# Delta rule's squared query and key lengths: two fp32r products of a rounded square and its remainder in place of one fp32 product

## What is computed

```python
def l2_norm(x):
    xf = x.astype(jnp.float32)
    return xf * lax.rsqrt(jnp.sum(xf * xf, axis=-1, keepdims=True) + EPS)
...
    qkv = jax.nn.silu(causal_depthwise_conv(jnp.concatenate([q_dn, k_dn, v_dn], axis=-1), w_conv))
    q_b, k_b, v_b = jnp.split(qkv, [DN_QK_W, 2 * DN_QK_W], axis=-1)
    q_b = l2_norm(q_b.reshape(bsz, seq, DN_HEADS, DN_KEY_DIM))
    k_b = l2_norm(k_b.reshape(bsz, seq, DN_HEADS, DN_KEY_DIM))
```

## Time and profile before

| what | value |
|---|---|
| median of 3 runs | 1245.12 us (1244.88 to 1246.83) |
| profiled execution, time | 1245.51 us |
| profiled execution, span of its instructions | 1243.8 us |
| PE busy | 1228.5 us (99%) |
| DVE busy | 688.9 us (55%) |
| ACT busy | 625.8 us (50%) |
| DMA, mean over the span | 123 GB/s |
| length loop: first sum to first key transpose | 599.10 to 630.68 us |

### The profile page before, as it was taken

How to read it: one execution, slowest core, us unless ns; L and a number is a source line. 1 busy time by engine, 2 the same in 40 slices (tenths; PEclk the granted TensorE clock), 3 DMA queues, 4 the chain that set the end, 5 groups by cost and what they waited for, 6 DMA issues and landing times.

```text
span 1243.8 us, 18228 instructions
## 1 busy us (share of the span) xinstructions
PE 1228.5 (99%) x6631; PEld 998.3 (80%) x6631; DVE 688.9 (55%) x997; ACT 625.8 (50%) x1144; POOL 65.5 (5%) x96
## 2 busy tenths in 40 slices
PE   7999999999999999999999999999999999999998
PEld 5788888888888787777788888877788888888887
DVE  4566666675665884887584565566733333332221
ACT  4577676775554766665864344453532233231221
POOL 0000000001110000000321210003000000000000
PEclk9999999999999999999999999999999999999999
DMA  9666665675553333212231223643233333343320
GB/s 351 193 204 184 202 197 174 181 222 161 161 154 103 84 90 81 68 51 69 61 93 49 56 69 102 191 148 96 72 104 101 92 93 101 101 117 105 110 84 26
DMA packets 278040, 152.41 MB, mean 123 GB/s; under 512 B 8006, under 2 KB 273375, under 8 KB 277983
## 3 DMA queue, kind: packets, MB, share of 16 engines
q1 hardware_dynamic: 273626, 149.49, 41.0%
q10 hardware_dynamic: 4356, 2.15, 0.6%
HBM read 145.31 MB, written 6.29 MB: 122 GB/s over the span
## 4 chain that ended last, share of the span: by engine, by line
PE 89%; ACT 3%; DVE 3%; DMA 3%; issue 1%; SPq 0%; DVEq 0%; ACTq 0%
PE region L1691 12%; PE region L1693 12%; PE region L1696 12%; PE tail L1691 8%; PE tail L1693 8%; PE tail L1696 8%; PE tail L1681 5%; PE tail L1683 5%; PE tail L1682 5%; DMA gates<-kept_gates 2%; PE region L1983 1%; DVE w_lo L1089 1%; PE region L2150 1%; PE region L2142 1%; DMA ada_early<-in_w_ada 1%
## 5 line engine op out<-in xcount | busy, mean ns | idle before, releaser
L601 ACT ACTIVATE w_hi<-raw 128x1024 fp32r<-128x1024 f32 (+1 forms) x177 | 197.3, 1115 | 409.2 <-PE region L1696 205.4
L1089 DVE TENSOR_TENSOR w_lo<-raw,w_hi 128x1024 fp32r<-128x1024 f32 (+1 forms) x176 | 229.2, 1302 | 202.7 <-ACT w_hi L601 201.9
L1691 PE MATMUL region<-u_hi,w_hi 128*128 128x512 f32 x640 | 158.8, 390 | 0.7 <-ACT w_hi L601 0.5
L1693 PE MATMUL region<-u_lo,w_hi 128*128 128x512 f32 x640 | 158.1, 389 | 0.0
L1696 PE MATMUL region<-u_hi,w_lo 128*128 128x512 f32 x640 | 158.1, 389 | 0.0
L1691 PEld LDWEIGHTS region<-u_hi,w_hi 128*128 128x128 f32 x640 | 119.9, 188 | 26.9 <-ACT w_hi L601 1.0
L1693 PEld LDWEIGHTS region<-u_lo,w_hi 128*128 128x128 f32 x640 | 120.2, 188 | 25.0
L1696 PEld LDWEIGHTS region<-u_hi,w_lo 128*128 128x128 f32 x640 | 120.1, 188 | 24.9
L621 ACT ACTIVATE ada_raw<-ada_raw,cond 128x128 f32<-128x128 f32 x448 | 134.1, 388 | 0.8 <-DMA ada_raw<-in_w_ada 0.8
L1681 PE MATMUL tail<-u_hi,w_hi 128*128 128x512 f32 x272 | 111.3, 409 | 2.2 <-DVE w_lo L1089 2.2
L1683 PE MATMUL tail<-u_hi,w_lo 128*128 128x512 f32 x272 | 106.3, 391 | 0.0
(11 more groups left out here) (371 smaller groups left out, 1639.2 us busy)
## 6 DMA issues: line engine op xcount, KB each, us to landing
raw<-in_w_ffn_in SPq DMA_DIRECT2D x168, 256.0 KB, 3.4
ada_raw<-in_w_ada SPq DMA_DIRECT2D x56, 512.0 KB, 4.6
raw<-in_w_in SPq DMA_DIRECT2D x90, 256.0 KB, 3.3
raw<-in_w_ffn_out SPq DMA_DIRECT2D x32, 384.0 KB, 4.5
raw<-in_w_ffn_out SPq DMA_DIRECT2D x32, 320.0 KB, 3.7
ada_early<-in_w_ada SPq DMA_DIRECT2D x8, 1024.0 KB, 9.7
gates<-kept_gates SPq DMA_DIRECT2D x16, 256.0 KB, 4.1
raw<-in_w_out SPq DMA_DIRECT2D x16, 256.0 KB, 3.3
```

The costliest lines, as they stand in the source:

```text
L601: act.activation(w_hi[:, slot % 2, 0:k, :], raw[:, slot, 0:k, :], ACT.Copy).then_inc(hi_ready, 1)
L1089: dve.tensor_tensor(w_lo[:, slot % 2, 0:k, :], raw[:, slot, 0:k, :], w_hi[:, slot % 2, 0:k, :].bitcast(f32), ALU.subtract).then_inc(lo_rea ...
L1691: pe.matmul(bank(b), w_hi[:, slot, n, :], x_hi[:, x0 + n, :], start=start and n == 0, stop=False)
L1693: pe.matmul(bank(b), w_hi[:, slot, n, :], x_lo[:, x0 + n, :], start=False, stop=False)
```

## The change

ACT rounds each square into an fp32r tile (`l2_hi`: `acc_hi` for even r, one half of a new tile `sq_pair` for odd r). DVE subtracts to get the remainder (`l2_lo`: `acc_lo`, or the other half of `sq_pair`). PE multiplies both by the fp32r ones and adds them up in the same bank. `acc_hi` and `acc_lo` served the modulation vector, whose last round is over by then.

```diff
--- before.py
+++ after.py
@@ -170,6 +170,7 @@
         gate_col = sb("gate_col", [P, 3, KD])
         ada_acc = sb("ada_acc", [P, 4, P])
         acc_hi, acc_lo = sb("acc_hi", [P, 4 * P], f32r), sb("acc_lo", [P, 4 * P], f32r)
+        sq_pair = sb("sq_pair", [P, 2, S], f32r)
         eps = sb("eps", [P, 1])
         share = sb("share", [P, 1])
         tok = sb("tok", [P, 4, NB])
@@ -259,6 +260,14 @@
         def sq_low(n):
 
             return att_hi.rearrange("p e n -> p (e n)")[:, (2 + n % 2) * S:(2 + n % 2) * S + S]
+
+        def l2_hi(r):
+
+            return sq_pair[:, 0, :] if r % 2 else acc_hi[:, :]
+
+        def l2_lo(r):
+
+            return sq_pair[:, 1, :] if r % 2 else acc_lo[:, :]
 
         def parts_of(s):
 
@@ -917,6 +926,8 @@
                     if r >= 2:
                         act.wait_ge(l2_stat, r - 1)
                     act.activation(work[:, r % 2, :], conv[:, L2[r], :], ACT.Square).then_inc(l2_sq, 1)
+                    act.wait_ge(l2_sq, r + 1)
+                    act.activation(l2_hi(r), work[:, r % 2, :], ACT.Copy).then_inc(half_hi, 1)
 
             for m in range(DNH):
                 both = (2 * m, 2 * m + 1)
@@ -1488,6 +1499,10 @@
             fill = filler(mixed)
             tmp = prod[:, 0].rearrange("p h e -> p (h e)")
             for m in range(DNH):
+                for r in (2 * m, 2 * m + 1):
+                    dve.wait_ge(half_hi, 2 * SBH + r + 1)
+                    dve.tensor_tensor(l2_lo(r), work[:, r % 2, :], l2_hi(r).bitcast(f32), ALU.subtract)\
+                        .then_inc(half_lo, 1)
                 fill("l2" if m else "silu")
                 for r in (2 * m, 2 * m + 1):
                     rs, cc = flat(link, r % 2), L2[r]
@@ -2050,10 +2065,12 @@
             for m in range(DNH):
                 fill("l2" if m else "silu")
                 for r in (2 * m, 2 * m + 1):
-                    pe.wait_ge(l2_sq, r + 1)
+                    pe.wait_ge(half_hi, 2 * SBH + r + 1)
                     if r >= 4:
                         pe.wait_ge(l2_rs, 3 * (r - 4) + 1)
-                    pe.matmul(bank(r % 4), ones[:, :], work[:, r % 2, :], start=True, stop=True).then_inc(l2_stat, 1)
+                    pe.matmul(bank(r % 4), ones_r[:, :], l2_hi(r), start=True, stop=False)
+                    pe.wait_ge(half_lo, 2 * SBH + r + 1)
+                    pe.matmul(bank(r % 4), ones_r[:, :], l2_lo(r), start=False, stop=True).then_inc(l2_stat, 1)
                 if m in (1, 2):
                     v_transposes(range(2 * m - 2, 2 * m))
             fill("start")
```

## The result

The changed kernel takes 1254.58 us (median of 6 runs, 1252.44 to 1255.74), the kernel before in the same session 1245.59 us (6 runs, 1244.70 to 1246.96). The ratio is 1.0066, 95% interval 1.0055 to 1.0076: 0.55 to 0.76% slower. The forecast was 1251.3 us with a range up to 1253.8; the measured median lies 0.8 us above the range. The profiled execution of the changed kernel, 1252.44 us with a span of 1250.7, was the quickest of the six, so its trace may show less of the loss than the median holds.

What follows compares the result with a forecast made beforehand. PE, busy 99%, was taken as the bound. Less PE work (-3.1 us), two old gaps gone (-1.0) and new standing (+10.2) made +6.1, so 1251.3 us, range 1248.5 to 1253.8.

Steps and rivals of the forecast that it cites:

- The wait: PE's second sum product waits for DVE's remainder: some 4 to 6 us in pass 1, 1 to 1.5 two or three times.
- PE's fourth product: Last sum product of pass 1, forecast to start at 613.9 us, with PE free at 614.13.
- pass 0: First pass of the length loop: PE free at 601.58 us against 600.82 before, a shift of +0.76.
- Pass 1: Second pass: PE arrives at 607.06 us, waits for remainders behind DVE's eight instructions, free at 614.13; shift +5.7, standing 6.1.
- passes 2 and 3: Last two loop passes: PE stands 1.3 us in each; shifts of +5.6 and +6.15 us.
- The price of work: Busy time: DVE's rises by 5.5 us for eight subtractions, ACT's by about 5 for eight copies; PE's falls.
- the term of the sum for the clock: The main case's +6.1 us held no loss for a falling clock; that was left to rival A.
- rival A: Clock falls in PE's gap of pass 1, work after 613.3 us slowed: about +1.7 us, 1253.0 us; chance 0.13.
- Rival B: Only pass 1 costs; the 2.6 us of standing in passes 2 and 3 goes: 1248.7 us; chance 0.12.
- Rival C: PE's sums meet no wait, so its 3.1 us saving reaches the end: 1242.0 us; chance 0.03.
- a microsecond taken off PE's list is gained: Premise from PE being busy 99% of the span at granted clock 1.00; time PE stands still is lost.
- near 635.3: When tile 6 is scaled, the condition for the key transposes, which PE was forecast to reach at 636.8 us.

Runs made afterwards that it cites:

- low_between: Changed kernel with DVE's two remainders of pass m + 1 placed between the two tiles of pass m: 1251.02 us, ratio 1.0037 to the kernel before.
- keep_warm: Changed kernel plus 21 PE products that nobody reads, in the waits of pass 1: 1251.30 us, ratio 1.0043 to the kernel before.
- before_fill: Kernel before with filler of 14 and 10 chunks in the loop in place of 12 and 8: 1245.90 us, ratio 1.0000.
- between_fill: low_between with filler of 14 and 10 chunks in place of 12 and 8: 1249.21 us, ratio 1.0025 to the kernel before.
- one_product: Kernel before with one fp32r product of the rounded square; no copy, no subtraction, remainder left out of the sum: 1245.61 us, ratio 0.9992.
- one_split_between: one_product with the filler's w_lo between the two tiles of a pass on DVE: 1249.57 us, ratio 1.0030 to the kernel before.
- one_root_fill: one_split_fill with ACT taking logarithm and exponential tile by tile: 1242.67 us, ratio 0.9974 to the kernel before.
- no_low: Changed kernel without DVE's eight subtractions; PE's second product takes the rounded square again: 1246.89 us, ratio 1.0007 to the kernel before.
- one_split_fill: one_split_between with filler of 14 and 10 chunks in place of 12 and 8: 1246.14 us, ratio 1.0005 to the kernel before.
- low_free: Changed kernel with DVE's subtractions made but PE not waiting for them, its second product taking the rounded square: 1249.91 us, ratio 1.0031.

## Why the prediction missed

**What held.** The wait is where it was forecast, and for its reason: PE's second product of pass 1 waits for a remainder that stands on DVE behind the eight Newton and scaling instructions (low_between, which only moves the subtractions, takes 2.8 us off that wait). The times were close: Newton 607.00 forecast, 606.39 measured; first remainder of pass 1 begun at 612.57, measured 611.96; PE's fourth product 613.9, measured 613.72, of which 0.4 us is the slow clock (613.30 on the same count in keep_warm, whose loop begins 0.93 us later). The four passes, by their waits: pass 0 +0.76 forecast; in the trace PE needs 2.25 us from its first sum to the next filler (598.89 to 601.14) against 1.72, after a wait of 0.21, +0.7. Pass 1: 6.1 of standing forecast, 4.09 + 1.37 in the rows, some 0.6 more in the distance from 606.35. Keep_warm has the passes without the fall of the clock. Counted as in the forecast, from PE's arrival to its being free less 0.94, it stands 6.1 us in pass 1 (607.51 to 614.57) and 1.4 in passes 2 and 3 each (0.99 in the brackets), against 6.1, 1.3 and 1.3. Altogether waits and savings make +6.0 us in its profiled loop and +5.3 by its medians, against +6.1 forecast. The price of work was right as well: DVE +5.1 us (5.5 forecast), ACT +4.6 ("about 5").

**What failed** is the term of the sum for the clock: it was put at nothing, and left to rival A with a chance of 0.13: "the clock falls in the gap of pass 1". It did, and belonged in the main case; the runs put it at 1.5 us in the profiled loop and 3.3 us by the medians. One step led away from it: "no slice shows the lower level of 1.2 GHz", and the clock row says 1.00 from 6 to 8 us, so the 421 ns of the earlier trace rows were put down to something else. They were the evidence. After the gap the same shape of matmul takes the same time, now at a granted clock of 0.50 (614 to 616 us):

```profile
L2061 PE MATMUL region<-ident,conv x8: 415/421/421, 614.1 to 615.6; 128*128 128x128 f32 x8
```
The pace agrees: eleven such matmuls start in 2.1 us at the start of the program, eight in 1.56 us after the gap, eight in 0.80 us in pass 2. So the duration was the better sign and the clock row at the start most likely wrong, and between two readings I went by the one that suited the forecast. A's price, +1.7 us, was worked out as work of 3 us slowed to half, less 1.3 us of standing in pass 2 that would be free cover. In the profiled execution that is nearly what happened: three sums, eight transposes and six filler products, which take 0.7 + 0.8 + 1.4 = 2.9 us at 2.4 GHz, took from 612.70 to 618.41, 5.7 us, and the wait of 0.99 us in pass 2 went in return. PE was free after the sums of pass 2 at 623.68, in keep_warm at 623.25. Keep_warm's loop began 0.93 us later in its span (599.82 against 598.89), so 1.4 us were left of it. At the key transposes it is 1.5. So for the profiled execution A's price was nearly right.

By the medians keep_warm is 3.3 us faster, twice that, and the other executions of the changed kernel are slower than the profiled one: their mean clock over the span was 0.994 to 0.997 against 0.997, and 1255.74 us (at 0.994) is the highest. 0.003 of 1250 is 3.8 us of PE's clock, and highest and lowest are 3.3 us apart. Not all of that need lie in the loop, since the clock also falls elsewhere and without the change. In the experiments the kernel before ran 52 of its 95 executions at a mean clock of 1.000, 1245.3 us on average, and nine at 0.997, 1248.0 us. One place is in the traces: near 424 us PE stands 1.88 to 1.93 us for a `w_lo` in all sixteen. From 424 to 430 us the clock is then 1.00 in eleven of them, among them the two kernels compared and keep_warm, and 0.72 in five (before_fill, between_fill, one_product, one_split_between, one_root_fill). How much of the remaining 2 us is such falls, how much a longer fall in the loop, and how much noise (the intervals leave 0.7 to 5 us for the whole), stays open, since only one execution of a kernel is profiled. It also means that differences of 2 or 3 us between medians hold some of these falls.

The Trainium skill, page "TensorE: Matmul & The Clock Gate", section Part 1, says that an idle stretch of the array brings its clock back to half until sustained work raises it. This trace agrees (0.50 from 612 to 618 us after a gap of 6 us, 1.00 again from 624).

**Rival B**, only pass 1 costs: the profiled execution looks a little like it, no wait in pass 2 and one of 1.14 in pass 3, but for the clock's reason and not for B's; with the clock up the waits are there. **Rival C** rested on a sentence that the forecast also made in the main case: "a microsecond taken off PE's list is gained". One_product refutes it. It meets no remainder at all, saves 5.0 us and gains at most 2.1 (the interval's lower end, 0.9983); no_low, with two fp32r products and no remainder to wait for, gains nothing. The reason stood in my own reading of the earlier trace rows, "DVE is nearly as full here as PE": with tile 6 scaled 1.2 us ahead of the key transposes, a shorter loop on PE runs into DVE's after 1.2 us. The forecast asked for that condition after the change ("near 635.3") and never before it. So no more than 1.2 of the 3.1 us for less work on PE could have been had. It did no harm to the sum, since the new standing was counted as PE's arrival against DVE's chain and took it back, but C's 1242.0 us was some 2 us too low.

## What to carry to other kernels

A page on which one engine is busy 99% does not say that a microsecond off it is gained: in the stage that is changed, see how long before it the other engines are ready (here 1.2 us at the key transposes); more than that can't be gained while their lists stay as they are. Before giving an in-order engine one more instruction for which another engine waits, read what stands ahead of it there; and if PE stands still for microseconds, price what it does next at half the clock too. Where two engines hand tiles to each other, the order of the steps (one_root_fill against one_split_fill: 3.5 us, a fall of the clock among them) can matter more than the price of any one.

## What was not expected of the hardware

The clock went down after quite short stops, and not alike. PE stood for 2.2 us in no_low and ran at 0.58 of full speed from 608 to 612 us; in low_free, with the same stop (605.99 to 608.23), it stayed at 1.00 in the profiled execution. The stop of 1.9 us near 424 us, the same in sixteen traces, went with 0.72 from 424 to 430 us in five of them and with 1.00 in the others. In one_split_fill a wait of 3.31 us brought it to 0.57, while after 1.88 us at the same place in one_root_fill it was 1.00. Five microseconds of products that nobody reads made the kernel 3.3 us faster by the medians. And the clock row of a profile is not proof of full speed: from 6 to 8 us it reads 1.00 while 128x128 fp32 matmuls take 421 ns, as they do at 0.50 later, and 272 ns at 1.00.
